# A two-block layer on one core: recurrence side products regrouped, norms passed on tile by tile, last half banks split

## What is computed

```
q_dec = q * exp(b);  k_inv = k * exp(-b)
o_intra = (q_dec k_inv^T, causal) v
S[n+1] = exp(b_last) * S[n] + (k * exp(b_last - b))^T v
o = o_intra + q_dec S[n];   then rms_norm(o) * silu(gate)
```

## Time and profile before

| | |
|---|---|
| Median of 3 runs | 1447.51 us (1447.35 to 1455.02) |
| The profiled execution | 1447.28 us |
| Its span, first to last instruction | 1445.5 us |
| PE busy | 1425.1 us, 99% |
| DVE, ACT, POOL busy | 966.7, 734.4, 209.6 us |
| Mean granted TensorE clock | 0.998 of 2.4 GHz |

### The profile page before, as it was taken

How to read it: one execution, slowest core, us unless ns; L and a number is a source line. 1 busy time by engine, 2 the same in 40 slices (tenths; PEclk the granted TensorE clock), 3 DMA queues, 4 the chain that set the end, 5 groups by cost and what they waited for, 6 DMA issues and landing times.

```text
span 1445.5 us, 25160 instructions
## 1 busy us (share of the span) xinstructions
PE 1425.1 (99%) x10271; PEld 1290.1 (89%) x10271; DVE 966.7 (67%) x1746; ACT 734.4 (51%) x1055; POOL 209.6 (14%) x120
## 2 busy tenths in 40 slices
PE   8999999999999999999999999999999999999998
PEld 7989979999999999998777778888899888899986
DVE  5565674693944777778888876655577864677754
ACT  5673654545454444444444445544567754555543
POOL 5000000488883000000000000000014100000000
PEclk9999999999999999999999999999999999999999
DMA  6433446455555545555555566555443453455553
GB/s 237 145 131 102 162 161 210 140 179 186 180 186 178 172 162 172 165 163 173 175 164 172 168 223 240 186 184 185 160 152 122 152 180 108 158 178 187 187 184 111
DMA packets 66931, 245.07 MB, mean 170 GB/s; under 512 B 7424, under 2 KB 7552, under 8 KB 66560
## 3 DMA queue, kind: packets, MB, share of 16 engines
q1 hardware_dynamic: 66816, 243.45, 50.5%
HBM read 242.37 MB, written 1.05 MB: 168 GB/s over the span
## 4 chain that ended last, share of the span: by engine, by line
PE 93%; ACT 3%; DVE 2%; issue 1%; POOL 1%; DMA 0%; SPq 0%; DVEq 0%; POOLq 0%; ACTq 0%
PE bank L427 92%; ACT A L1038 1%; ACT whi L1038 1%; PE bank L436 1%; DVE wlo L1548 1%; ACT L1038 1%; DVE A L1548 0%; DVE A L1544 0%; DMA raw<-in_w_in_t 0%; POOL wlo L2347 0%; POOL small L2353 0%; DVE xres L1551 0%; DVE xres L1548 0%; ACT hTh L1038 0%; DVE hTl L1551 0%
## 5 line engine op out<-in xcount | busy, mean ns | idle before, releaser
L1548 DVE TENSOR_TENSOR wlo<-raw,whi 128x1024 fp32r<-128x1024 f32 x374 | 457.9, 1225 | 334.0 <-ACT whi L1038 333.5
L1038 ACT ACTIVATE whi<-raw 128x1024 fp32r<-128x1024 f32 x448 | 472.9, 1057 | 403.9 <-PE bank L427 402.5
L427 PE MATMUL bank<-hTh,whi 128*128 128x256 f32 x1944 | 555.2, 286 | 2.3 <-DVE wlo L1548 1.0
L427 PE MATMUL bank<-hTh,wlo 128*128 128x256 f32 x1944 | 548.8, 282 | 0.0
L427 PE MATMUL bank<-hTl,whi 128*128 128x256 f32 x1944 | 547.2, 281 | 0.0
L427 PEld LDWEIGHTS bank<-hTh,whi 128*128 128x128 f32 x1944 | 366.4, 188 | 6.9 <-DVE hTl L1551 2.5
L427 PEld LDWEIGHTS bank<-hTl,whi 128*128 128x128 f32 x1944 | 367.0, 189 | 0.3 <-issue 0.2
L427 PEld LDWEIGHTS bank<-hTh,wlo 128*128 128x128 f32 x1944 | 364.9, 188 | 0.0
L427 PE MATMUL bank<-whi,hTh 128*128 128x512 f32 (+2 forms) x552 | 218.3, 396 | 0.2
L2347 POOL TENSOR_TENSOR wlo<-raw,whi 128x1024 fp32r<-128x1024 f32 x74 | 177.3, 2398 | 274.9 <-ACT whi L1038 271.0
L427 PE MATMUL bank<-wlo,hTh 128*128 128x512 f32 (+2 forms) x552 | 215.0, 390 | 0.0
(11 more groups left out here) (171 smaller groups left out, 1373.4 us busy)
## 6 DMA issues: line engine op xcount, KB each, us to landing
raw<-in_u SPq DMA_DIRECT2D x128, 512.0 KB, 3.3
raw<-in_v SPq DMA_DIRECT2D x128, 512.0 KB, 3.3
raw<-in_w_up SPq DMA_DIRECT2D x44, 512.0 KB, 3.3
raw<-in_w_down SPq DMA_DIRECT2D x22, 512.0 KB, 3.3
raw<-in_w_in_t SPq DMA_DIRECT2D x18, 512.0 KB, 4.2
raw<-in_w_in_g SPq DMA_DIRECT2D x16, 512.0 KB, 3.3
raw<-in_w_out SPq DMA_DIRECT2D x16, 512.0 KB, 3.8
raw<-in_w_pq SPq DMA_DIRECT2D x16, 512.0 KB, 3.5
```

Source lines behind the costliest of these rows:

```text
L427: return e.matmul(o, l, r, start=st, stop=sp_, skip_group_check=True)
L1038: return e.activation(o, i, func, **kw)
L1548: return e.tensor_tensor(o, a, b, op)
```

## The change

Four things change.

1. **Recurrence.** The side products of `hgrn` are put into more and smaller groups: at middles of units the increments 0, 2, 4, 6, then inner 1, outputs 3 and 4, output 7; at ends the increments 1, 3, 5, then inner 0, outputs 1 and 2, outputs 5 and 6. Everything behind them (mean products, Ln, Exp, `yhT`) comes two steps later, on all three engines. `late_gates` is not changed.
2. **Heads.** `norm_head` takes the place of `norm_pe` and of the first two units at j = 0, 1 and 5: eight transposes of block 0, four of block 1, then two filling products, then a loop over the eight tiles that does each tile's products of both first units, with one of the other four transposes ahead of it. ACT and DVE split tile by tile (`norm_hi_tiles`, `norm_lo_tiles`). At j = 1 and 5 ACT scales block 0 (`scaled0`), DVE block 1. The fillers are 4, 1, 2 (0, 1, 2 at the start).
3. **Last half bank.** In `lin_A` of `w_out`, `w_xo` and `w_down` the last half (512 columns) of the last two units becomes two parts of 256 columns, the second into the first bank, which is free by then. DVE adds 512 columns after the first part (`acc2`, `r_part`) and 256 after the second, and squares the last 256 itself (`part_add_and_sum`).
4. **Bridge.** ACT makes `whi` of the third `w_xk` unit before the bridge's first step instead of after it, and DVE sums both blocks' squares before it scales the first one.

```diff
+PARTS = {0: 1, 3: 2, 4: 3}
+SCALED = (0, 8, 12, 20, 28, 36)
+SCALED0 = {1: 0, 5: 4}
...
+            def norm_tile(j, src, b, k):
+                if k % 2 == 0:
+                    if b == 0 and j in SCALED0:
+                        e.wait_ge(s["n_scaled0"], SCALED0[j] + k // 2 + 1)
+                    else:
+                        e.wait_ge(s["n_scaled"], SCALED[j] + (4 * b if j not in SCALED0 else 0) + k // 2 + 1)
+                o = (k // 4 * 2 + b) * P
+                ins = tr(banks[k % 4][:, o:o + P], src[:, b * D + k * P:b * D + (k + 1) * P])
+                if b:
+                    ins.then_inc(s["n_tr"], 1)
+            def norm_head(j, src, u0, spins):
+                for b in range(TB):
+                    if spins[b]:
+                        spin(spins[b], 7)
+                    for k in range(8 if b == 0 else 4):
+                        if b == 0 and k < 4:
+                            use(k)
+                        norm_tile(j, src, b, k)
+                bk = 4 + pair[0] % 3
+                use(bk)
+                wa, wb = (two(unit(u0 + i), KD) for i in range(2))
+                spin(spins[2], 7)
+                for k in range(KD):
+                    e.wait_ge(s["n_lo"], 8 * j + k + 1)
+                    if k < 4:
+                        norm_tile(j, src, 1, k + 4)
+                    h = [z[:, k, :] for z in hTv]
+                    ins = three(banks[bk][:, 0:256], [z[:, k, :] for z in wa], h, k == 0, k == KD - 1)
+                    if k == KD - 1:
+                        ins.then_inc(s["w"], 1)
+                    ins = three(banks[bk][:, 256:512], [z[:, k, :] for z in wb], h, False, k == KD - 1)
+                ins.then_inc(s["w"], 1)
...
             def hgrn_mid():
-                for n in (0, 2, 4):
+                for n in (0, 2, 4, 6):
                     hgrn_rec(n)
                     yield
-                hgrn_rec(6)
-                hgrn_out(1)
-                hgrn_out(2)
-                yield
-                hgrn_out(5)
-                hgrn_out(6)
+                hgrn_inner(1)
+                yield
+                hgrn_out(3)
+                hgrn_out(4)
+                yield
+                hgrn_out(7)
                 yield
...
-                hgrn_rec(1)
-                yield
-                hgrn_rec(3)
+                for n in (1, 3, 5):
+                    hgrn_rec(n)
+                    yield
                 hgrn_inner(0)
                 yield
-                hgrn_rec(5)
-                hgrn_inner(1)
-                yield
-                hgrn_out(3)
-                hgrn_out(4)
-                yield
-                hgrn_out(7)
+                hgrn_out(1)
+                hgrn_out(2)
+                yield
+                hgrn_out(5)
+                hgrn_out(6)
+                yield
                 yield
                 yield
...
-            norm_pe(1, scr, spins=(4, 2))
-            lin_T(BASE["w_pq"], 16, hTv, KD, normed(1, 4))
+            norm_head(1, scr, BASE["w_pq"], (4, 1, 2))
+            lin_T(BASE["w_pq"] + 2, 14, hTv, KD)
...
+            def scaled0(r, dst):
+                e.wait_ge(s["n_rstd"], 2 * r + 1)
+                for c in range(4):
+                    act(dst[:, c * 256:c * 256 + 256], xres[:, c * 256:c * 256 + 256], ACT.Copy, scale=small[:, 2:3]
+                        ).then_inc(s["n_scaled0"], 1)
...
-                for _ in range(5):
+                for _ in range(7):
                     yield
...
             hi(0)
-            norm_hi(0, "g_mix", hTv, 0)
             hi(1)
-            for k2 in range(1, 4):
-                norm_hi(0, "g_mix", hTv, k2)
+            norm_hi_tiles(0, "g_mix")
...
-            residual_squares(0, scr)
+            part_squares(0, scr)
+            scaled0(1, scr)
             hi(BASE["w_pq"] + 1)
-            for k2 in range(4):
-                norm_hi(1, "g_ffn", hTv, k2)
+            norm_hi_tiles(1, "g_ffn")
...
             side.lists[0].append(bridge())
+            hi(BASE["w_xk"] + 2)
             side.step()
-            lin_T(BASE["w_xk"], 6, copy_to(kT2))
+            side.step()
+            hi(BASE["w_xk"] + 3)
+            e.wait_ge(s["w"], BASE["w_xk"] + 2)
+            copy_to(kT2)(0, t3(banks[4 + pair[0] % 3][:, :], 2))
+            pair[0] += 1
+            side.step()
+            lin_T(BASE["w_xk"] + 2, 4, copy_to(kT2, 2))
...
+                tt(z, banks[b0 + 3][:, :], z, ALU.add).then_inc(s["r_part"], 1)
+                z = xres[:, D + 768:2 * D]
+                e.wait_ge(s["w"], last)
+                e.wait_ge(s["r_part"], PARTS[at])
+                tt(z, banks[b0][:, 0:256], z, ALU.add).then_inc(s["r_add"], 1)
+                e.wait_ge(s["r_add"], 4 * at + 4)
+                own(stt(scratch[:, D + 768:2 * D], z, 1.0 / D, z, ALU.mult, ALU.mult, accum_out=small[:, 8:9]))
...
                 final_scale(3, gfin, 1)
                 rms_sum(4, 0)
+                rms_sum(4, 1)
                 scaled(4, xres, scr3, 0)
-                rms_sum(4, 1)
...
-            add_and_sum("w_down", 0, NU, 7)
+            part_add_and_sum("w_down", 0, NU, 7, xs)
             e.wait_ge(s_gf2, 16)
             final_scale(7, gfin2, 0)
-            rms_sum(7, 1)
             final_scale(7, gfin2, 1)
...
-            e.wait_ge(s["n_scaled"], 16)
+            e.wait_ge(s["n_scaled"], 12)
             lo(BASE["w_pq"] + 1)
```

More of the change, by code:

```diff
@@ new lines, in norm_head @@
+            def norm_head(j, src, u0, spins):
[20 more added lines that the diff above has]
+                ins.then_inc(s["w"], 1)
+                for k in range(4):
+                    free[k] = (s["n_lo"], 8 * j + 4 + k + 1)
+                by, n_ev = PAIR_FREED[pair[0]]
+                free[bk] = (s[by], n_ev)
+                pair[0] += 1
@@ L472, in lin_T, with normed @@
+            def normed(j):
+                return lambda k: e.wait_ge(s["n_lo"], 8 * j + 2 * (k // 2) + 2) if k % 2 == 0 else None
             def lin_T(u0, units, src, K, first=None, after=None, steps=(1,)):
@@ L497, in lin_T, with lin_A @@
                     side.step(steps[(i + 1) % len(steps)])
-            def lin_A(u0, src, K, N, bks, ready, pair=True):
+            def lin_A(u0, src, K, N, bks, ready, pair=True, split=None):
                 per, nh = UNIT // N, N // 512
@@ L529, in lin_A @@
                     block(units - 1, 1, wb, 0).then_inc(s["acc1"], 1)
-                    block(units - 2, 1, wa, 1).then_inc(s["w"], 1)
-                    block(units - 1, 1, wb, 1).then_inc(s["w"], 1)
+                    if split is not None:
+                        for c in range(2):
+                            if c:
+                                e.wait_ge(s["r_add"], 4 * split + 1)
+                            o = banks[bks[0]][:, 0:256] if c else banks[bks[3]][:, 0:256]
+                            for k, wv in ((K - 2, wa), (K - 1, wb)):
+                                ins = three(o, [z[:, k, P:2 * P] for z in src],
+                                            [z[:, 0, 512 + 256 * c:768 + 256 * c] for z in wv], c == 1 and k == K - 2,
+                                            k == K - 1)
+                                if c:
+                                    ins.then_inc(s["w"], 1)
+                            if not c:
+                                ins.then_inc(s["acc2"], 1)
+                        for i, (by, n) in enumerate((("r_add", 4 * split + 4), ("r_add", 4 * split + 2),
+                                                     ("r_add", 4 * split + 3), ("r_part", PARTS[split]))):
+                            free[bks[i]] = (s[by], n)
+                    else:
+                        block(units - 2, 1, wa, 1).then_inc(s["w"], 1)
+                        block(units - 1, 1, wb, 1).then_inc(s["w"], 1)
                 else:
@@ L1023, in head_ready @@
                 e.wait_ge(s["cr_dve"], 6 * (h // 2) + 5 + h % 2)
-            lin_A(BASE["w_xo"], oT2, KD, D, (4, 5, 6, 7), head_ready)
-            for i in range(4):
-                free[4 + i] = (s["r_add"], 12 + i + 1)
-            norm_pe(5, xs, spins=(4, 2))
-            lin_T(BASE["w_up"], 44, hTv, KD, normed(5, 4))
-            lin_A(BASE["w_down"], aF, 22, D, (0, 1, 2, 3), lambda k: e.wait_ge(s["ff_lo"], k + 1))
+            lin_A(BASE["w_xo"], oT2, KD, D, (4, 5, 6, 7), head_ready, split=3)
+            norm_head(5, xs, BASE["w_up"], (4, 1, 2))
+            lin_T(BASE["w_up"] + 2, 42, hTv, KD)
+            lin_A(BASE["w_down"], aF, 22, D, (0, 1, 2, 3), lambda k: e.wait_ge(s["ff_lo"], k + 1), split=4)
         def act_program(e):
@@ L2183, in dve_program @@
             e.wait_ge(s_keep, 16)
-            for k2 in range(4):
-                norm_lo(0, "g_mix", hTv, k2)
+            norm_lo_tiles(0, "g_mix")
             l0, l1 = C1("lb", 0, 4), C1("lb", 4, 8)
@@ L2234, in dve_program @@
             lin_A(BASE["w_out"], 8, hold=True)
-            residual_norm("w_out", 0, BASE["w_out"] + 8, 1, scr)
-            for k2 in range(4):
```

(3 more changed lines are left out.)

83 lines of the change are left out of this document (57 added, 26 removed).

## The result

The changed kernel takes 1459.43 us (median of 14 runs, 1457.42 to 1461.14), the kernel before 1447.97 us in the 14 runs beside it. The ratio on record is 1.0068 with a 95% interval of 1.0056 to 1.0081 (it uses all runs, three of which took 1454.7 to 1455.0 us before; the medians alone give 1.0079). The changed kernel is slower, by 11.5 us in the medians and 10.0 in the means, more than the 0.5% that this kernel's measurement can tell. The prediction said 1457.3 us, 1448 to 1462, and gave "slower" the largest chance. The profiled execution took 1459.22 us with a span of 1457.4 us, so it is compared with the profiled 1447.28 us of before.

What follows compares the result with a forecast made beforehand. PE, busy 99% of the span, was taken to bound the kernel. Terms 2.9 + 1.5 + 1.5 + 0.1 + 0.1 + 0 + 3.1 - 2.4 + 3.0 = +9.8 us on 1447.28 gave 1457.1, as median 1457.3; range 1448 to 1462.

Steps and rivals of the forecast that it cites:

- Heads: Before `w_pq` and `w_up`: PE waits for POOL's second-unit split, transposes stand in the loop; +1.5 us each, bounds +0.7 to +2.0.
- Start: Kernel's first head: first product at 13.6 instead of 11.38, later tiles delay unit 2's split; +2.9 us, bounds +2.0 to +3.3.
- Clock: PE standing still at the heads lets the clock fall, 1.5 us at two of three places; +3.0 us, bounds 0 to +6.
- Gates: Between `w_in_g` and `w_hp`: four ACT table loads and later `yhT` make PE wait; +3.1 us, bounds 0 to +4.
- (b): Between `w_in_g` and `w_hp`: ACT's four loads stay covered, `w_hp` starts on time; 1454.2 us, without the clock 1451.2; chance 0.17.
- Regrouping: Recurrence's side products in new groups: PE's work the same, costed at nothing; +0.24 us if each new group costs a transpose's return.
- Bridge: Before `w2_t`: earlier `whi` frees POOL, final scaling starts 2.2 us earlier; -2.4 us, bounds -1.5 to -2.9.
- Splits and tail: Three split ends, 12 products of 256 columns for 6 of 512: +0.1 us together; kernel's tail gains nothing: +0.1.
- (a): All heads: the clock holds, as PE's fillers and transposes are enough; sum +6.8, 1454.3 us; chance 0.20.
- (c): The heads win, if POOL's second-unit `wlo` is ready before the first low tile; 1443.9 us; chance 0.13.
- (d): The clock falls at all three heads and for longer; 1461 us; chance 0.10.

Runs made afterwards that it cites:

- x_dve_split: Changed kernel with the second unit's low part at the three heads made by DVE, ahead of the low tiles, instead of POOL: median 1451.18 us, ratio 1.0013.
- x_gap_moved: Changed kernel with the two empty steps of ACT's late_gates put after the sixth Sigmoid instead of the fourth: median 1457.4 us, ratio 1.0058.
- x_fill_ahead: Changed kernel with the fillers put ahead of the wait for the two splits and made more (18, 12, 12 instead of 2): median 1452.11 us, ratio 1.0019.

## Why the prediction was right, and where not

- **Heads (+1.5 each, before the clock).** POOL's split was to run until 213.75; it ran from 219.35 to 221.70, and 221.70 less the 7.97 us by which `w_out` started later is 213.73. Every link held. The wait itself costs 0.92, against 1.0 for the 1.5 without the two fillers. In the profiled execution a head took +2.7, as the clock fell as well, and the two fillers behind the wait ran at half the rate.
- **Start (+2.9).** The first product came at 13.42, predicted 13.6. Unit 2 came at 22.45 where 20.75 was said: DVE's split began at 20.68 instead of 19.5, as tiles 4 to 7 were transposed at 1.2 GHz, and took about 1.7 us instead of 1.25, a term that was not in the sum. With the clock held and the fillers ahead of the wait the start costs 1.94: there DVE's eighth tile was done at 16.9 (17.6 in the sum) and the split of unit 2 ran from 18.50 to 19.7. The 2.9 had 0.5 for the two fillers in it, so what is left, 2.4, was 0.5 too much.
- **Clock (+3.0, two of three places at 1.5).** This is the step that was mis-sized. It fell at all three heads, and with the fillers behind the waits this is worth 6.2 us, against 3.0 plus 1.5 for the fillers in the forecast. The reading of the earlier trace rows was right: standing still for 2.5 us was enough, as 2.1 had been at the end, while the 1.24 us at the heads of x_dve_split were not. A fourth fall, in the mixer (+1.3), was not in the sum.
- **Gates (+3.1).** Measured +3.26. The third `w_ap` split of DVE ended at 174.17, less the 4.61 of the start 169.56, where the prediction had 169.55; `R1l` ended at 176.97 on that scale, predicted 177.15. The two parts, up to the third unit of `w_ap` and from there to `w_hp`, are 1.6 and 1.65, predicted 1.4 and 1.7; of both together the loads' order makes 1.95, as x_gap_moved showed. Rival (b), loads that stay covered, fell.
- **Regrouping (0).** The groups moved nothing that the traces show at full clock. What was not seen is that with the old ones an execution sometimes takes 6 to 11 us more, 9.3 in the one that was traced. The one profile of before had no such fall; the spread of its three runs (1447.35 to 1455.02) was the only sign, and the prediction did not use it.
- **Bridge (-2.4).** Measured -2.7. In the changed kernel:

```profile
1048.15 2.50 POOL L2460 TENSOR_TENSOR wlo<-raw,whi 128x1024 fp32r<-128x1024 f32 x1 [140.02 <-ACT whi L1090]
1050.69 0.55 POOL L2466 TENSOR_TENSOR small<-small 128x1 f32<-128x1 f32 x1
...
1052.13 1.41 DVE L1632 SCALAR_TENSOR_TENSOR xres<-xres,small,A 128x512 f32<-128x512 f32 x2
...
1059.61 1.53 DVE L1625 TENSOR_SCALAR A<-xres,small 128x256 f32<-128x256 f32 x4
```

  Less the 10.68 us of this place, POOL ends at 1039.97 (predicted 1039.9) and the final scaling starts at 1041.45 (1041.5). The last scaling starts at 1048.9 (1049.4) and takes 1.53 us where the earlier trace rows had 1.97; POOL's masks stand beside 0.9 us of it and stood beside 1.8. So it ends 2.7 us earlier, which is the whole gain: 2.3 by its start and 0.4 by its length. The prediction had 1.8 for the start; the 0.6 that its 2.4 needs beyond that is not worked out there.
- **Splits and tail (+0.1 each).** The last products of `w_out`, `w_xo` and `w_down` come 0.11 to 0.13 us later each, 0.36 together where 0.1 was said. Behind the last product the kernel takes 7.03 us, before 7.10, so the tail cost nothing. Another 0.1, between the first products of `w_hp` and `w_out`, comes with the later `yhT` and was not in the sum.
- **Rivals.** (a), a clock that holds, is what the version with the fillers ahead shows: 1452.1, where 1454.3 was said, since the fillers don't stand behind the wait (1.5) and the start is 0.5 cheaper. (c) needed POOL's split to be early. It never was, but the heads win 0.6 each as soon as the first unit doesn't ask for it. (d), falls at all three heads, had the mechanism that happened, with the chance of 0.10, and its 1461 is nearer to 1459.4 than the forecast's 1457.3; but 1.3 of the measured time is the mixer's fall, which neither has, and without it 1458.1 is nearer to the forecast. The parts that the prediction gives for "slower" by 0.5% (0.40, 0.10, two fifths of 0.20 and a little of (b)) add up to more than the 0.57 that it states, to 0.58 and that little.

By its parts the changed kernel's loss is: start 4.6, gates 3.3, `w_hp` 0.1, heads 5.4 (0.2 of it two of the split ends), the third split end 0.1, mixer 1.3, bridge -2.7, together 12.1 against 12.0 measured at the last product. So the mechanisms were right and the total is right in part by luck: the waits of the heads and the start cost 3.8 us where 4.4 was said, and the bridge gained 0.3 more, which took back some of the clock's 1.7 and the mixer's 1.3.

## What to carry to other kernels

A loop that does two units' products tile by tile waits for the slower of their two splits; let the first unit run on its own operands and only the order of its tiles be finer. Fillers belong ahead of a wait: those of x_fill_ahead lasted until it ended and held the clock, while two behind it added their own time and did not. When a step moves by k units, write down each engine's queue at the new place: a table load or a wait for another engine that lands ahead of a weight's split can make PE wait for it (1.95 and 3.7 us here), whether it moved there or stayed while the rest moved. And a spread among the runs of before is a row too: 7.5 us in one run of three was a cost that the profiled execution did not show.

## What the runs showed that was not expected

The granted clock fell to 1.2 GHz in three kinds of place. After 2.5 us of standing still at a head it stayed there for 3.41 us, at a net cost of 1.7 to 1.8 us with the fillers; at the start, after 3.8 us, it was 2.7. (In other runs a fall at the start lasted 6.83 us.) In the second block's mixer it fell for 3.41 us in eight of the twelve profiled executions with PE busy: ahead of it in the changed kernel were 16 products of 128 x 128 in float32, then eight on 4 rows with one of bf16 among them, 4.6 us from 1118.32 on. The kernel before has the same products from 1110.35 on, and its profiled execution kept its clock. Nothing in the edits goes with the fall, and its cause stays open. And once it fell for 20.48 us behind groups of up to 24 small products, 8 on 32 rows and 16 with 32 columns, at 9.3 us; what in them does it is open. A busy PE row is no proof of a full clock.
